# Gate columns of an mLSTM folded into the rotary key's weight unit of a three-branch mixer

## The reference, cut to what matters

```python
z = x @ w_in
(c_q, c_kv, k_r, mq, mk, mv, mi, mf, mo, rq, rk, rv, rg, gl) = _split_cols(z, IN_SPLITS)
gates = jnp.concatenate([mi, mf], axis=-1) + mlstm_gate_b
i_pre, f_pre = gates[..., :MLSTM_HEADS], gates[..., MLSTM_HEADS:]
lf = log_sigmoid(f_pre); g = cumsum(lf)          # per chunk of 128 tokens
k_rope = _rope(k_r[:, :, None, :], pos)[:, :, 0, :]
```

## Time and profile before

| | before |
|---|---|
| time, median of 3 runs | 1362.99 us (1362.76 to 1364.14) |
| time of the profiled execution | 1363.81 us |
| its span | 1361.5 us |
| TensorE busy | 1343.3 us (99%) |
| VectorE busy | 931.2 us (68%) |
| ScalarE busy | 651.7 us (48%) |
| conversions on VectorE / ScalarE | 221 of 2.26 us / 221 of 1.88 us mean |

### The profile page before, as it was taken

The page is one execution under the profiler, slowest core; times in us unless marked ns, Lnnn a source line. Parts: engine busy times, 40 slices in busy tenths (PEclk is TensorE's granted clock), DMA queues, the critical chain, the costliest instruction groups (busy, mean ns, idle before and its releaser), DMA issues.

```text
span 1361.5 us, 19494 instructions
## 1 busy us (share of the span) xinstructions
PE 1343.3 (99%) x8456; PEld 1199.3 (88%) x8456; DVE 931.2 (68%) x1015; ACT 651.7 (48%) x667; POOL 66.0 (5%) x59
## 2 busy tenths in 40 slices
PE   7999999999999999999999999999999999999998
PEld 7888889998999988888888888899989999888886
DVE  5665567898985575555675555768999657765555
ACT  4444446485554444444454444545746444444442
POOL 2970000000000000000000000000000000000000
PEclk9999999999999999999999999999999999999999
DMA  8555555444355545656556555456434555555552
GB/s 301 186 187 187 187 183 164 144 154 125 124 156 186 185 149 192 186 188 190 178 180 191 186 185 186 147 159 187 125 115 134 186 186 171 169 186 186 185 186 93
DMA packets 178244, 234.63 MB, mean 172 GB/s; under 512 B 5808, under 2 KB 152880, under 8 KB 178032
## 3 DMA queue, kind: packets, MB, share of 16 engines
q1 hardware_dynamic: 177920, 231.68, 53.4%
q0 software_dynamic: 240, 1.71, 0.3%
HBM read 232.33 MB, written 1.05 MB: 171 GB/s over the span
## 4 chain that ended last, share of the span: by engine, by line
PE 96%; DVE 3%; ACT 1%; DMA 0%; issue 0%; DVEq 0%; SPq 0%
PE ps L1362 21%; PE ps L1373 21%; PE ps L1298 13%; PE ps L1300 12%; PE ps L1299 12%; PE ps L1361 9%; PE ps L1365 1%; PE ps L1518 1%; PE ps L1320 1%; DVE xpair L860 1%; PE ps L1327 1%; PE ps L1536 1%; DVE xf L872 1%; PE ps L1556 1%; PE ps L1566 1%; PE ps L1561 1%
## 5 line engine op out<-in xcount | busy, mean ns | idle before, releaser
L779 DVE TENSOR_TENSOR wlo<-raw,whi 128x2048 fp32r<-128x2048 f32 (+3 forms) x221 | 493.9, 2258 | 133.7 <-ACT whi L490 133.5
L490 ACT ACTIVATE whi<-raw 128x2048 fp32r<-128x2048 f32 (+3 forms) x221 | 414.8, 1879 | 171.4 <-DMA raw<-ffn_w_gate 114.4
L1362 PE MATMUL ps<-xpair,whi 128*128 128x512 f32 x1216 | 422.3, 397 | 0.0
L1361 PE MATMUL ps<-xpair,wlo 128*128 128x256 f32 x1064 | 296.9, 279 | 0.0
L1298 PE MATMUL ps<-xpair,whi 128*128 128x256 f32 (+1 forms) x960 | 274.9, 286 | 0.0
L1299 PE MATMUL ps<-xpair,whi 128*128 128x256 f32 (+1 forms) x960 | 271.6, 283 | 0.0
L1300 PE MATMUL ps<-xpair,wlo 128*128 128x256 f32 (+1 forms) x960 | 271.6, 283 | 0.0
L1362 PEld LDWEIGHTS ps<-xpair,whi 128*128 128x128 f32 x1216 | 220.6, 188 | 42.7
L1361 PEld LDWEIGHTS ps<-xpair,wlo 128*128 128x128 f32 x1064 | 200.6, 189 | 6.9
L1298 PEld LDWEIGHTS ps<-xpair,whi 128*128 128x128 f32 (+1 forms) x960 | 179.6, 187 | 2.8 <-issue 1.2
L1299 PEld LDWEIGHTS ps<-xpair,whi 128*128 128x128 f32 (+1 forms) x960 | 179.7, 187 | 2.2 <-issue 1.0
(11 more groups left out here) (227 smaller groups left out, 1726.4 us busy)
## 6 DMA issues: line engine op xcount, KB each, us to landing
raw<-w_in SPq DMA_DIRECT2D x60, 1024.0 KB, 5.2
raw<-ffn_w_up SPq DMA_DIRECT2D x44, 1024.0 KB, 5.4
raw<-ffn_w_down SPq DMA_DIRECT2D x44, 1024.0 KB, 4.9
raw<-ffn_w_gate SPq DMA_DIRECT2D x43, 1024.0 KB, 5.4
raw<-w_br SPq DMA_DIRECT2D x12, 1024.0 KB, 5.1
raw<-w_out SPq DMA_DIRECT2D x8, 1024.0 KB, 4.8
raw<-mla_w_uq SPq DMA_DIRECT2D x4, 576.0 KB, 3.9
raw<-mla_w_ukv SPq DMA_DIRECT2D x2, 1024.0 KB, 4.9
```

The source lines that it names most:

```text
L490: act.activation(whi[:, n % RING, 0:size_of(n)], raw[:, n % RING, 0:size_of(n)], ACT.Copy).then_inc(w_hi, 1)
L779: dve.tensor_tensor(w_low(n), raw[:, n % RING, 0:size_of(n)], whi[:, n % RING, 0:size_of(n)].bitcast(F32), ALU.subtract).then_inc(w_lo, 1)
L1361: pe.matmul(ps[:, bank, 0:SEQ], wl[:, kk, cols], xhi[:, kk, :], start=False, stop=False)
L1362: last = pe.matmul(ps[:, bank, :], wh[:, kk, cols], xpair[:, kk, :, :], start=kk == 0, stop=kk == KC - 1)
```

## The change

The c2 unit gets 228 columns: the old 192, then 32 columns of `w_in` from the first gate column on (four input gates, four forget gates, 24 columns that nobody reads), then the four forget gate columns once more. So the second c2 call, which had 64 output rows, has 100: rows 0 to 63 are the rotary key, 64 to 67 the input gates, 96 to 99 the forget gates. It comes by three DMAs with a semaphore of their own. The gate unit and its projections are gone; every later unit of the mixer has a number one lower, while the places `hi(m0+13)`, `lo(m0+13)` and so on keep theirs, so each place now converts the unit after the one it had. ScalarE adds the biases while it copies the gate rows out, right after the copies of c2, and qk3 waits for that. The banks of the later projections move by one, and `lo(m0+14)` moves from ahead of scores(0) to behind probs(1). Lines that change only in a unit's number, and the shifted bias columns in the parameters, are left out:

```diff
-MIX_FIXED, MIX_LOOP, MIX_OUT = 23, 18, 4
+MIX_FIXED, MIX_LOOP, MIX_OUT = 22, 18, 4
+C2 = 228
+    def load_no(n):
+        own = [l * U_LAYER + MIX_BASE + 4 for l in range(DEPTH)]
+        return n // RING + 1 - sum(c <= n and c % RING == n % RING for c in own)
...
-            "gates", "rq0", "rq1", "rk0", "rk1", "rv0", "rv1", "mo0", "mo1", "rg0", "rg1"]
+            "rq0", "rq1", "rk0", "rk1", "rv0", "rv1", "mo0", "mo1", "rg0", "rg1"]
-    GATE_BANK, BRANCH_BANK = (5, 6), (7, 4)
+    GATE_BANK, BRANCH_BANK = (4, 5), (6, 7)
...
-            load_in(l, 4, 512, 192)
+            n = m0 + 4
+            sp.wait_ge(w_used, done_no(n - RING))
+            dst = raw[:, n % RING, 0:KC * C2].rearrange("p (a b) -> p a b", a=KC)
+            for c0, lo, width in ((0, 512, 192), (192, C_GATES, 32), (C2 - HEADS, C_GATES + HEADS, HEADS)):
+                sp.dma_start(dst[:, :, c0:c0 + width], chunks(a["w_in"][l, :, lo:lo + width]))\
+                  .then_inc(c2_loaded, 16)
-            load_in(l, 12, C_GATES, 2 * HEADS)
...
-            act.wait_ge(w_loaded[n % RING], (n // RING + 1) * 16)
+            if n % U_LAYER == MIX_BASE + 4:
+                act.wait_ge(c2_loaded, (n // U_LAYER + 1) * 48)
+            else:
+                act.wait_ge(w_loaded[n % RING], load_no(n) * 16)
...
             last.then_inc(rot_copied, 1)
+            act.activation(row_i[:, :], ps[ROPE:ROPE + HEADS, BANK["c2"], SEQ:], ACT.Identity,
+                           bias=par_col(l, "i_b", 0)[ROPE:ROPE + HEADS, :])
+            act.activation(row_f[:, :], ps[96:96 + HEADS, BANK["c2"], SEQ:], ACT.Identity,
+                           bias=par_col(l, "f_b", 0)[96:96 + HEADS, :]).then_inc(f_pre, 1)
             hi(m0 + 8)
...
-            hi(m0 + 46)
...
-            lo(m0 + 14)
             scores(0)
             scores(1)
-            gbank = ps[0:HEADS, BANK["gates"], :]
-            dve.wait_ge(w_used, done_no(m0 + 12))
-            dve.tensor_scalar(row_i[:, :], gbank[:, 0:SEQ], par_col(l, "i_b", 0)[0:HEADS, :], None, ALU.add)
-            dve.tensor_scalar(row_f[:, :], gbank[:, SEQ:], par_col(l, "f_b", 0)[0:HEADS, :], None,
-                              ALU.add).then_inc(f_pre, 1)
             dve.wait_ge(f_pre, l + 1)
             stt(row_t[:, :], row_f[:, :], -1.0, ALU.mult, row_f[:, :], ALU.max).then_inc(f_abs, 1)
             probs(0)
             probs(1)
+            lo(m0 + 14)
             conv(3)
...
-            lo(m0 + 46)
...
-            features(ps[:, BANK["c2"], 0:SEQ], m0 + 4, 192, slice(0, P), x_h, x_l, KC)
-            last = features(ps[0:ROPE, BANK["c2"], SEQ:], m0 + 4, 192, slice(P, 192), x_h, x_l, KC)
+            features(ps[:, BANK["c2"], 0:SEQ], m0 + 4, C2, slice(0, P), x_h, x_l, KC)
+            last = features(ps[0:C2 - P, BANK["c2"], SEQ:], m0 + 4, C2, slice(P, C2), x_h, x_l, KC)
...
-            pe.wait_ge(rot_copied, l * 6 + 1)
+            pe.wait_ge(f_pre, l + 1)
             project(8, "qk3")
...
-            pe.wait_ge(w_lo, done_no(m0 + 12))
+
+            pe.wait_ge(rotated, l * 6 + 2)
             pe.wait_ge(k_copied, l * 2 + 1)
-            for i in range(2):
-                last = features(ps[0:HEADS, BANK["gates"], i * SEQ:(i + 1) * SEQ], m0 + 12, 2 * HEADS,
-                                slice(i * HEADS, (i + 1) * HEADS), x_h, x_l, KC)
-            last.then_inc(w_used, 1)
-
-
-            pe.wait_ge(rotated, l * 6 + 2)
             mla_scores(0)
             mla_scores(1)
-            pe.wait_ge(k_copied, l * 2 + 2)
-            project(13, "rq0")
+            project(12, "rq0")
             mla_turn(0)
             pe.wait_ge(lat_std, l + 1)
             mla_turn(1)
-            pe.wait_ge(v_copied, l * 6 + 4)
-            project(14, "rq1")
+            pe.wait_ge(k_copied, l * 2 + 2)
+            project(13, "rq1")
...
-            project(15, "rk0")
+            pe.wait_ge(v_copied, l * 6 + 3)
+            project(14, "rk0")
...
-            pe.wait_ge(f_pre, l + 1)
-            project(16, "rk1")
+            pe.wait_ge(v_copied, l * 6 + 4)
+            project(15, "rk1")
```

More of the change, by code:

```diff
@@ L228, in build @@
     w_loaded = [sem(f"w_loaded{s}") for s in range(RING)]
+    c2_loaded = sem("c2_loaded")
     w_hi, w_lo, w_used = sem("w_hi"), sem("w_lo"), sem("w_used")
@@ L314, in half_no @@
         return (stage * TT + t) * 2 + half + 1
-    MIX_SIZE = ([2048] * 4 + [KC * 192] + [2048] * 4 + [QC * 384] * 2 + [VC * 1024]
-                + [KC * 2 * HEADS] + [2048] * (MIX_FIXED - 13 + MIX_LOOP + MIX_OUT))
+    MIX_SIZE = ([2048] * 4 + [KC * C2] + [2048] * 4 + [QC * 384] * 2 + [VC * 1024]
+                + [2048] * (MIX_FIXED - 12 + MIX_LOOP + MIX_OUT))
     def size_of(n):
@@ L416, in mixer @@
             load(m0 + 11, chunks(a["mla_w_ukv"][l, :, :]), (VC, 1024))
-            load_in(l, 12, C_GATES, 2 * HEADS)
-            for m, c in ((13, C_RQ), (15, C_RK), (17, C_RV), (19, C_MO), (21, C_RG)):
+            for m, c in ((12, C_RQ), (14, C_RK), (16, C_RV), (18, C_MO), (20, C_RG)):
                 for i in range(2):
@@ L426, in mixer @@
                     for i in range(2):
-                        load_in(l, 23 + 6 * b + 3 * h + i, C_GL + b * D_MODEL + 512 * h + 256 * i, 256)
-                    load(m0 + 25 + 6 * b + 3 * h, chunks(a["w_br"][l, b, :, 512 * h:512 * h + 512]), (HEADS, 512))
+                        load_in(l, 22 + 6 * b + 3 * h + i, C_GL + b * D_MODEL + 512 * h + 256 * i, 256)
+                    load(m0 + 24 + 6 * b + 3 * h, chunks(a["w_br"][l, b, :, 512 * h:512 * h + 512]), (HEADS, 512))
             for i in range(MIX_OUT):
-                load(m0 + 41 + i, chunks(a["w_out"][l, 256 * i:256 * i + 256, :]), (2, D_MODEL))
+                load(m0 + 40 + i, chunks(a["w_out"][l, 256 * i:256 * i + 256, :]), (2, D_MODEL))
         for l in range(DEPTH):
@@ L682, in mixer @@
             hi(m0 + 17)
-            act.wait_ge(w_used, done_no(m0 + 14))
+            act.wait_ge(w_used, done_no(m0 + 13))
             act.wait_ge(rotated, l * 6 + 3)
@@ L692, in mixer @@
             bc_copy(1)
-            act.wait_ge(w_used, done_no(m0 + 15))
+            act.wait_ge(w_used, done_no(m0 + 14))
             act.wait_ge(rotated, l * 6 + 4)
@@ L699, in mixer @@
             hi(m0 + 19)
-            act.wait_ge(w_used, done_no(m0 + 16))
+            act.wait_ge(w_used, done_no(m0 + 15))
             act.wait_ge(rotated, l * 6 + 5)
@@ L723, in mixer @@
             hi(m0 + 24)
-            act.wait_ge(w_used, done_no(m0 + 21))
+            act.wait_ge(w_used, done_no(m0 + 20))
             copy(flat(rg[:, 0:2, :]), "rg0", func=ACT.Silu).then_inc(rg_ready, 1)
             hi(m0 + 25)
-            act.wait_ge(w_used, done_no(m0 + 22))
+            act.wait_ge(w_used, done_no(m0 + 21))
             copy(flat(rg[:, 2:4, :]), "rg1", func=ACT.Silu).then_inc(rg_ready, 1)
@@ L1200, in mixer @@
             weigh(3)
-            dve.wait_ge(w_used, done_no(m0 + 18))
+            dve.wait_ge(w_used, done_no(m0 + 17))
             for t in range(TT):
@@ L1696, in mixer @@
             pe.wait_ge(rot_copied, l * 6 + 4)
-            values_half(17, ("rv0", "rv1"), 0)
+            values_half(16, ("rv0", "rv1"), 0)
             pe.wait_ge(bc_copied, l * 4 + 2)
@@ L1704, in mixer @@
             spread(3)
-            values_half(18, ("rv0", "rv1"), 1)
+            values_half(17, ("rv0", "rv1"), 1)
             pe.wait_ge(h_ready, l * 4 + 2)
@@ L1711, in mixer @@
             pe.wait_ge(rot_copied, l * 6 + 5)
-            project(19, "mo0")
+            project(18, "mo0")
             pe.wait_ge(bc_copied, l * 4 + 4)
@@ L1724, in mixer @@
             pe.wait_ge(rot_copied, l * 6 + 6)
-            project(20, "mo1")
+            project(19, "mo1")
             pe.wait_ge(h_ready, l * 4 + 4)
@@ L1731, in mixer @@
             ret_scores(3)
-            project(21, "rg0")
+            project(20, "rg0")
             pe.wait_ge(h_centred, l * 4 + 2)
@@ L1738, in mixer @@
             ret_values(1)
-            project(22, "rg1")
+            project(21, "rg1")
             for b in range(3):
@@ L1761, in mixer @@
                             variances(3)
-                    k = m0 + 25 + 6 * b + 3 * h
+                    k = m0 + 24 + 6 * b + 3 * h
                     pe.wait_ge(w_lo, done_no(k))
@@ L1784, in mixer @@
             for i in range(MIX_OUT):
-                k = m0 + 41 + i
+                k = m0 + 40 + i
                 pe.wait_ge(w_lo, done_no(k))
@@ L1827, in columns, with rows_as_column @@
         return np.asarray(v).reshape(DEPTH, -1, P).transpose(0, 2, 1)
-    def rows_as_column(v):
+    def rows_as_column(v, row):
         out = np.zeros((DEPTH, P, 1), np.float32)
-        out[:, :HEADS, 0] = v
+        out[:, row:row + HEADS, 0] = v
         return out
```

14 lines of the change are left out of this document (7 added, 7 removed).

## The result

The changed kernel takes 1355.49 us (median of 4 runs, 1355.03 to 1355.60), the kernel before 1363.38 beside it (4 runs, 1362.76 to 1364.14): 7.9 us less, a ratio of 0.9942 with an interval of 0.993 to 0.9955. The prediction was 1354.5, with a range of 1351.8 to 1357.5.

The account below looks back on a forecast made before the run. TensorE's own instruction stream was taken to set the time. Per layer -5.55 + 1.20 + 0.07 = -4.28 us, two layers -8.6, taken as -8.5 from the median 1362.99: 1354.5 us, range 1351.8 to 1357.5.

Parts of the forecast that it names:

- What goes: TensorE, ahead of the scores: 48 gate matmuls a layer vanish, 5.55 us a layer, 11.1 us for both.
- c2 wider: Second c2 call: 24 matmuls grow from 64 to 100 stationary columns, 0 to 0.14 us a layer, taken as 0.07.
- The biases and the split: ScalarE bias additions after c2's copies, at most 2 x 0.46 us, and 0.3 us more VectorE split: taken as hidden.
- The loads: c2's three-piece load: at most 9.0 us against 20.6 us available after issue, so hidden.
- Where the time comes back: VectorE's queue through the soft-max delays probs(3); TensorE waits 1.2 us a layer at the fourth head's transposes.
- Afterwards: Behind the soft-max: VectorE catches up, the rest shifts rigidly; one-unit-later load holds ScalarE at most 5.8 us once, no charge.
- The sum: Whole kernel: -4.28 us a layer, -8.6 for two layers, taken as -8.5, giving a median of 1354.5 us.
- A: Rival, chance 0.12: TensorE never waits in the mixer and all the removal arrives, 11.0 us, 1352.0 us.
- B: Rival, chance 0.12: later loads or the key SiLU add 1 to 2 us of waits a layer, 1356.5 to 1358.5 us.
- C: Rival, chance 0.03: moved lo(m0+14) in the soft-max chain delays probs(3) by 4.35 us more, leaving no gain.
- D: Rival, chance 0.03: c2's narrow loads land late, over 20.6 us after issue; 30 us would give 1373 us.

Follow-up runs that it names:

- e4: Changed kernel with lo(m0+14) moved behind conv(3) and lo(m0+16) moved behind probs(3): 1352.59 us, ratio 0.9921.
- e7: Kernel before with only the gate projections cut to the first of eight chunks, 6 matmuls instead of 48 a layer: 1356.29 us, ratio 0.9947.
- e5: Changed kernel with c2's 32-column piece loaded as eight pieces of four columns: 1355.63 us, ratio 0.9942.
- e3: Changed kernel with only lo(m0+16) moved behind probs(3): 1353.53 us, ratio 0.993.
- e8: Changed kernel with a useless 2.27 us VectorE maximum added behind the gate rows, ahead of lo(m0+16): 1361.95 us, ratio 0.999.
- e2: Changed kernel with lo(m0+14) moved one place later, behind conv(3): 1355.23 us, ratio 0.9941.
- e1: Changed kernel with lo(m0+14) put back ahead of scores(0): 1355.28 us, ratio 0.9942.
- e9: Kernel e4 with a useless 2.27 us VectorE maximum added behind the gate rows, ahead of y_mla(0): 1355.29 us, ratio 0.9944.

## Why the prediction was right, point by point

- **What goes.** Shown. The earlier trace rows gave 5.55 us a layer; e4, which has no new wait, gains 5.47 in the stretch. e7, without the rest of the change, is 7.1 us faster than the kernel before in its batch (1356.29 against 1363.41), so the removed matmuls are the cause and not the new unit. The Trainium skill's isolated gap of columns/2.4 + 2.5 ns ("TensorE: Matmul & The Clock Gate", Back-to-back issue gap) would make the removal 48 x 109 ns = 5.2 us a layer, an estimate; the stretch of e4 is 5.47 shorter, so the trace does not agree with it here.
- **c2 wider.** The term was 0.07 us a layer, measured 0.08 (2.82 against 2.74).
- **The biases and the split.** Hidden as taken: 0.47 us each on ScalarE, no wait of TensorE at qk3 in the view of waits.
- **The loads.** Hidden as taken, and with room: e5 needs 11.3 us for ten pieces and the time does not move. The Trainium skill warns of transfers below 512 bytes ("DMA: Bandwidth & Descriptors", Specifications); 128 and 16 byte rows landed in 5.2 and 4.8 us, beside 4.6 for 768 KB. That is slow for their size, so the trace agrees with the page, and still far from the 20.6 us at which it would be felt. The prediction's sentence that 2.2 us for the 32-byte rows contradict it holds for the lateness of the load, not for the page.
- **Where the time comes back.** This was the step that carried the forecast: 1.20 us a layer, at the second pair's transposes, partly ahead of the first values. Measured 1.28: 0.52 at the values (e3 against e4) and 0.76 at the fourth head (the kernel after against e3). The VectorE times were met within 0.08 us. That the sum was met as closely is in part luck: the queue ended 0.08 us earlier than added up (297.46 for 297.54), and the fourth head's transposes start 0.23 us behind that point (297.69), a hand-over that the prediction took as nothing. The idle that the profile lists is only 0.30 + 0.56 = 0.86; the other 0.42 lies in the rows around the waits and goes with them in e4. The cause is shown from two sides: taking a conversion out of the queue and putting conv(3) first gives the time back (e3, e4), adding an operation takes as much again (e8, layer 1). Moving a conversion inside the queue does nothing (e2); in e1 it does nothing either, but the loss comes at the first pair.
- **Afterwards.** VectorE caught up and the rest of the mixer shifted rigidly, as taken. The load that comes one unit later held ScalarE 4.63 us (bound 5.8). It was not "once": ScalarE waits for loads again behind it, and VectorE for ScalarE 1.61 us in all (the prediction said 1) out of the 4.16 it had. TensorE lost nothing: the whole distance from layer to layer is 671.26 - 665.86 = 5.40 us shorter in e4, the stretch's 5.47 less the 0.08 of c2, which leaves no room for a loss there.
- **The sum.** -4.28 a layer was predicted; the distance from layer to layer shrank by 4.07 and the stretch by 4.19. Of the 0.21 us a layer between 4.28 and 4.07, 0.08 are VectorE's queue, 0.07 the scores, 0.01 c2; the rest is unassigned. The forecast for the median was -8.5, measured -7.9; between spans -8.2.
- **Rivals.** A (all arrives) did not happen in this order, and does in e4's: 1352.59 against the 1352.0 that it named. B (more given back) would need waits behind 360 us; the view of waits has none. C (the conversion overtakes the gain): in e1 and e2 its place makes no difference to the time, and e8 shows in layer 1 that VectorE's time comes through one for one, so that some 4 us more of it in each layer would be needed to reach the time of before. D (narrow loads) fell with e5.

Not settled: why the clock fell behind the wait in one layer of e8 and not in the other, and why the first row of the scores costs 0.07 us more. That row is listed with 0.38 us where gate matmuls stand ahead of it (before, e7) and with 0.46 where the values' do (after, e1, e3, e4).

## What to carry to other kernels

When work is taken out of the engine that bounds the kernel, what arrives is the removal less what its producers cannot follow: walk the producer's queue from the place of the removal to the next hand-over and add up the rows; here that gave 1.2 us of 5.55, and 1.28 were measured. Then look in that queue for work that is not wanted before the hand-over. Moving it from one place to another ahead of the hand-over did nothing (e1, e2), moving it behind gave 0.76 us of the loss back (e3), and with what a second, earlier hand-over needs put first as well, all of it (e4: 1352.59 instead of 1355.49).

## What the runs showed of the hardware

- **A wait of TensorE costs about 0.2 us more than its listed idle time.** Against e4, which has none of them, the stretch is 0.52 us longer for one wait of 0.28 (e3), 1.28 for two of 0.86 in sum (after), 1.30 for 0.90 (e1), 1.31 for 0.91 (e9), and 136.53 - 133.05 = 3.48 for three of 2.87 in sum (e8, layer 1): 0.20 to 0.24 us a wait on top. Most of it is how a row is listed: the matmul ahead of the values has 0.28 us and is followed after 0.12 in a stream, so 0.16 us of the standstill lie under it. The rest is in the row behind, 0.67 us after a wait and 0.59 in e4.
- **A wait of 2.02 us was followed by a lower clock in one of two identical places**: 3.02 us instead of 1.88 for the four spreads, granted clock 0.50 for the three microseconds from 300 to 303. In the mixers of the other kernels no wait is longer than 0.81 us (e7), and the clock behind them was 1.00.
- **The width of the stationary operand shows a little in the spacing** of fp32r matmuls with 256 moving columns: 114 ns with 64 columns, 117.5 with 100, 120 with 128, but 116 with four.
- **Many-row loads with rows of 16 bytes were cheap to add here**: nine of them, 1024 rows each, land in 3.2 us (median), and the ten issues take 8.75 us of the queue, about 0.9 us each. It costs nothing here because that queue has the time.
